# The order of five TensorE parts in a recurrence step: scores and masked product ahead of the state's product and the updates

## The reference, cut to what matters

```python
b_c = jnp.cumsum(_chunk(log_f), axis=3)
u = jnp.einsum('bhnck,bhncv->bhnkv', k_end, v_c)              # update of each chunk
s_next = d_n[..., None] * s + u_n                             # the state's chain over chunks
o_inter = jnp.einsum('bhnck,bhnkv->bhncv', q_c * jnp.exp(b_c), s_prev)
a = jnp.einsum('bhnck,bhnsk->bhncs', q_c * jnp.exp(b_c - b_mid), k_c * jnp.exp(b_mid - b_c))
a = jnp.where(jnp.tril(jnp.ones((CHUNK, CHUNK), dtype=bool)), a, 0.0)
o_intra = jnp.einsum('bhncs,bhnsv->bhncv', a, v_c)
return (o_inter + o_intra).reshape(b, h, t, -1)
```

## Time and profile before

| | |
|---|---|
| device time, median of 3 runs | 2343.97 us (2338.73 to 2344.09) |
| span of the profiled execution | 2340.7 us |
| PE busy | 2222.3 us, 95% |
| DVE busy | 1327.2 us, 57% |
| ACT busy | 864.2 us, 37% |
| POOL busy | 463.9 us, 20% |

### The profile page before, as it was taken

One profiled execution on the slowest core, in us unless ns is written; L12 is line 12 of the kernel. 1 busy time (PEld: TensorE's weight loads), 2 busy tenths in 40 slices (PEclk: granted clock), 3 DMA queues, 4 the chain that ended last, 5 costly groups with the idle time before them and its releaser, 6 DMA issues.

```text
span 2340.7 us, 33900 instructions
## 1 busy us (share of the span) xinstructions
PE 2222.3 (95%) x12064; PEld 1436.2 (61%) x12258; DVE 1327.2 (57%) x2357; ACT 864.2 (37%) x1888; POOL 463.9 (20%) x439
## 2 busy tenths in 40 slices
PE   5799999999999999999999999999999999998998
PEld 2566667666667666666666766656655555554554
DVE  6747547537637628628627727755554546364444
ACT  5734334334334424424424424444432221314221
POOL 2021221222222222222212221000043213100100
PEclk7899999999999999999999999999999999999999
DMA  6210110110011011010011010243321111113443
GB/s 256 83 39 28 35 39 28 33 41 28 26 46 30 26 43 33 26 43 32 22 46 35 21 46 21 84 160 130 132 72 36 62 41 41 50 41 131 135 135 117
DMA packets 106775, 144.80 MB, mean 62 GB/s; under 512 B 7136, under 2 KB 74224, under 8 KB 105584
## 3 DMA queue, kind: packets, MB, share of 16 engines
q1 hardware_dynamic: 99648, 125.72, 16.5%
q10 hardware_dynamic: 6960, 16.80, 1.9%
HBM read 108.91 MB, written 33.57 MB: 61 GB/s over the span
## 4 chain that ended last, share of the span: by engine, by line
PE 76%; DVE 9%; issue 8%; ACT 5%; DMA 1%; POOL 1%; SPq 0%; DVEq 0%; POOLq 0%; ACTq 0%
PE bank L1213 22%; PE bank L1211 21%; PE bank L1212 19%; DVE w_st L1040 2%; PE bank L1337 2%; PE bank L1445 2%; PE bank L1332 2%; PE bank L1352 2%; PE bank L1363 1%; PE bank L1305 1%; DVE xa L997 1%; ACT xb L667 1%; DVE qp L981 1%; DMA ada_sb<-in_ada_w 1%; ACT xb L681 1%
## 5 line engine op out<-in xcount | busy, mean ns | idle before, releaser
L1213 PE MATMUL bank<-h_hi,w_lo 128*128 128x512 f32 (+1 forms) x1472 | 815.9, 554 | 0.0
L1211 PE MATMUL bank<-h_hi,w_hi 128*128 128x512 f32 (+1 forms) x1472 | 578.9, 393 | 8.6 <-issue 7.1
L1212 PE MATMUL bank<-h_lo,w_bf 128*128 128x512 bf16 (+1 forms) x1343 | 505.2, 376 | 4.9 <-issue 4.9
L1212 PEld LDWEIGHTS bank<-h_lo,w_bf 128*128 128x128 bf16 x1472 | 142.0, 96 | 334.8 <-issue 318.3
L1211 PEld LDWEIGHTS bank<-h_hi,w_hi 128*128 128x128 f32 x1472 | 282.4, 192 | 39.2 <-issue 9.8
L1213 PEld LDWEIGHTS bank<-h_hi,w_lo 128*128 128x128 f32 x1472 | 297.8, 202 | 5.2 <-issue 5.2
L1213 PE MATMUL bank<-wo_hi,og_lo 128*128 128x512 f32 x512 | 299.4, 585 | 0.0
L649 ACT ACTIVATE xa<-bank 128x512 f32<-128x512 f32 (+1 forms) x144 | 82.5, 573 | 398.6 <-PE bank L1213 398.6
L1213 PE MATMUL bank<-h_hi,pw_lo_b 128*128 128x512 f32 x384 | 222.8, 580 | 0.0
L1211 PE MATMUL bank<-wo_hi,og_hi 128*128 128x512 f32 x512 | 205.2, 401 | 12.2 <-DVE wo_lo L1086 7.1
L1040 DVE SCALAR_TENSOR_TENSOR w_st<-w_st,cv,bank 128x128 f32<-128x128 f32 x560 | 193.4, 345 | 19.0
(11 more groups left out here) (163 smaller groups left out, 3807.2 us busy)
## 6 DMA issues: line engine op xcount, KB each, us to landing
w_raw<-in_w_in SPq DMA_DIRECT2D x80, 256.0 KB, 2.8
ada<-in_ada_late SPq DMA_DIRECT2D x128, 128.0 KB, 2.1
ada_sb<-in_ada_w SPq DMA_DIRECT2D x8, 1024.0 KB, 12.6
xt<-in_x SPq DMA_DIRECT2D x16, 512.0 KB, 6.5
gated_scratch<-o_t ACTq DMA_DIRECT2D x32, 256.0 KB, 2.4
og<-gated_scratch SPq DMA_DIRECT2D x16, 512.0 KB, 4.1
xr<-in_x SPq DMA_DIRECT2D x16, 512.0 KB, 4.9
x_scratch<-xr ACTq DMA_DIRECT2D x16, 512.0 KB, 2.6
```

What stands on the lines that cost most here:

```text
L1211: pe.matmul(out_ap, hi, m_hi, start=start, stop=False)
L1212: pe.matmul(out_ap, bf, m_lo, start=False, stop=False)
L1213: return pe.matmul(out_ap, lo, m_hi, start=False, stop=stop)
```

## The change: another order on PE

In a step PE's order becomes projection, T, A, M, O, U, output transposes. The scores are issued right behind the transposes. The masked product goes ahead of the state's product, so it now starts bank OB's accumulation (`start=(j == 0)`) and the state's product ends it (`stop=True`, and `o_done` behind it). Each part keeps its own waits: A's for the last masked copy, M's for its own masked copy and for bank OB to be read, O's for `q2` and the chain. No other engine's instructions change.

```diff
                         last.then_inc(s["kt_tr"], 1)
+                        if lat(fi) is not None:
+                            ai = lat(fi)
+                            need(pe, "a_masked", NA, h, ai)
+                            for j in range(4):
+                                last = pe.matmul(bank[AB][:, j * P:(j + 1) * P], kp[:, fi % 2, j * P:(j + 1) * P],
+                                                 qp[:, ai % 2, j * P:(j + 1) * P], start=(j == 0), stop=True,
+                                                 skip_group_check=True)
+                            last.then_inc(s["a_done"], 1)
                     fi = st - (F0 + 4)
...
+                        need(pe, "a_masked", NA, h, ai + 1)
+                        need(pe, "o_read", NA, h, ai)
+                        o = bank[OB]
+                        for j in range(4):
+                            pe.matmul(o[:, j * P:(j + 1) * P], am[:, 2 * d + ai % 2, j, :],
+                                      v_tok[:, 2 + 4 * b + j, :], start=(j == 0), stop=False,
+                                      skip_group_check=True)
                         need(pe, "q2_ready", NA, h, ai + 1)
                         need(pe, "w_step", NCHAIN, h, chain_steps(fi) - 1)
-                        need(pe, "o_read", NA, h, ai)
-                        o = bank[OB]
                         for n in range(8):
...
-                            pe.matmul(o[r, c // 2 * P:(c // 2 + 1) * P], q2[:, ai % 2, c * CHUNK:(c + 1) * CHUNK],
-                                      w_st[:, (8 * ai + n) % 16, :], start=(n < 2), stop=False,
-                                      skip_group_check=True)
-                        need(pe, "a_masked", NA, h, ai + 1)
-                        for j in range(4):
-                            last = pe.matmul(o[:, j * P:(j + 1) * P], am[:, 2 * d + ai % 2, j, :],
-                                             v_tok[:, 2 + 4 * b + j, :], start=False, stop=True,
+                            last = pe.matmul(o[r, c // 2 * P:(c // 2 + 1) * P],
+                                             q2[:, ai % 2, c * CHUNK:(c + 1) * CHUNK],
+                                             w_st[:, (8 * ai + n) % 16, :], start=False, stop=True,
                                              skip_group_check=True)
                         last.then_inc(s["o_done"], 1)
...
-                    fi = st - (F0 + 2)
-                    if 0 <= fi < NF:
-
-                        if lat(fi) is not None:
-                            ai = lat(fi)
-                            need(pe, "a_masked", NA, h, ai)
-                            for j in range(4):
-                                last = pe.matmul(bank[AB][:, j * P:(j + 1) * P], kp[:, fi % 2, j * P:(j + 1) * P],
-                                                 qp[:, ai % 2, j * P:(j + 1) * P], start=(j == 0), stop=True,
-                                                 skip_group_check=True)
-                            last.then_inc(s["a_done"], 1)
```

## The result

The changed kernel takes 2360.95 us (median of 4 runs, 2357.94 to 2361.86), the kernel before on the same chip 2344.03 us: a ratio of 1.0073, interval 1.006 to 1.0087. It is 17 us slower. I had said 2348.5 us, 2338 to 2359, and gave "slower" 0.36; the result lies outside the range on the slow side. The profiled execution has a span of 2355.8 us (2357.94 us of device time), 15.1 us more than the span before.

What follows compares the result with a forecast made beforehand. PE was taken to bound the run most of the time, with DVE's state chain holding it in places. A head sums to 0.73 - 0.6 + 0.45 = +0.58 us, eight to +4.6, on 2343.97: 2348.5 us, range 2338 to 2359.

Steps and rivals of the forecast that it cites:

- slower: The outcome of a time above 2351 us, with 0.3% (7 us) counted as no change; chance 0.36.
- The new wait: A waits for DVE's masked copy, starting 1.05 us later than O did; steps 14 and 15 cost +0.73 us a head.
- Fewer changes of shape: In a full step PE changes the array's shape three times instead of four, saving 0.22 us.
- O to U is free: Rival: PE's change of shape from O to U costs nothing; 2337.3 us, or 2335 with DVE freed; chance 0.12.
- Step 20: Its end comes +0.45 us later a head, between 0.14 (0.8 us of DVE freed) and 0.95 (DVE keeps its pace).
- U's later result "is hidden": U's result comes some 1 us later, but DVE starts the chain more than 5 us behind it, so no cost.
- The layers behind the heads are as before: The layers after the eight heads stay unchanged, except that they start later by the heads' sum, +4.6 us.
- The clock ... I take 0: The low clock behind step 14's longer idle time adds 0 us in sum, range -3 to +7.
- The first rival: Long low clock behind step 14 in all heads, +7 us, and DVE's pace kept in step 20, +4: 2359.5; chance 0.2.

Runs made afterwards that it cites:

- run with the wait alone: The kernel before, with the state's product O also waiting for the last masked copy in steps that have scores; 2360.79 us, ratio 1.0085.
- the run with extra work: The changed kernel with twelve extra matmuls in step 14 of each head, ahead of the scores' wait for the masked copy; 2347.66 us, ratio 1.0008.
- the scores first: The kernel before with only the scores A moved behind the transposes, O still ahead of M (order T, A, O, M, U); 2354.61 us, ratio 1.0044.
- the early copy alone: The kernel before with only DVE's masked copy moved ahead of the state's chain; 2351.06 us, ratio 1.0036.

## Why the prediction was wrong, point by point

- **The new wait: right.** A in step 14 starts 0.05 us behind the copy's end, O never waits for the chain, A(19) comes 9.88 us behind projection 18 (I said 9.9). Up to step 16 the heads cost +6.6 us in sum (3.9 + 5.5 - 2.8) against a forecast of 8 x 0.73 = 5.8. The wait in step 13 I had overlooked; it is taken up by the idle time of step 14. The run with the wait alone loses 18 us with nothing moved, so the wait carries a loss of this kind without the order.
- **Fewer changes of shape: right in size.** O before U takes 1.02 us, as one paid change (I had 1.03); the rival "O to U is free" falls. By the Trainium skill's rule ("TensorEngine Tiling (Array Packing)", Key Properties) a change of mode drains the engine, and the trace agrees in that half columns to half rows is paid as whole to half is. Step 16 saved 0.19 us (T(16) to T(17), 9.56 to 9.37) and step 17, which has all five parts, 0.18, where I had 0.22 for each.
- **Step 20: the lower bound held.** I took +0.45 us a head between 0.14 and 0.95. PE does not wait in step 20: the masked copies of steps 18 and 19 are 8.14 us apart where they had been 10.91, since POOL's `q2` starts at 964.00, 4 us behind the copy of step 18 (959.99), where it had followed at 2 us. T(19) to the next head's T costs 8.4 us less 1.1 for each end, so next to nothing.

```profile
959.99 0.72 DVE L1049 COPY_PREDICATED am<-mask,bank 128x512 f32<-128x512 uint8 x1
...
968.13 0.73 DVE L1049 COPY_PREDICATED am<-mask,bank 128x512 f32<-128x512 uint8 x1
```
```profile
964.00 1.58 POOL L555 TENSOR_TENSOR q<-qp,cv 128x512 f32<-128x512 f32 x1 [18.15 <-PE bank L1345]
```

- **U's later result "is hidden": not quite.** DVE's chain waits 12.0 us over 16 times for U in the changed kernel, since A, M and O run at the low clock ahead of it; in the run with extra work, where the clock stays up there, it waits 1.8 us over 8 times. It does not reach PE, which waits for nothing in step 15.
- **"The layers behind the heads are as before", and no term for the heads' ends: the step that failed.** I had read step 22 as T to T and O against M, saw the saving of 0.03 us and stopped there. The jump's idle time, 1.5 to 2.1 us in the trace of before with the engine waiting for nothing that the profile names, was before me, and so was the low clock behind two of five ends. I took the idle time as fixed and the term as nothing. In the two profiles the idle time grew by 0.7 us each (3.5 us), and the time behind it, with the low clock, by 9.9 us: 13.4 of the 15.1 us. The two runs that change the last part alone measured 5.5 and 6 to 8 us, which is about half of the distance from my 2348.5 to 2360.95. The rest of the 13.4 us lies at the same place in the two profiles, and its cause stays open.
- **"The clock ... I take 0": the same fault.** I had weighed the clock only behind step 14, where it did stay nearly the same (+2 us, forecast 0, range -3 to +7). The first rival gave 2359.5 us for a different place: a long low stretch behind every step 14 and DVE's pace kept in step 20, neither of which happened. The time came close to that rival by luck, from another cause.
- **What is left.** Without the jump the sum would have been +1.7 us in the profile (15.1 - 13.4), against my +4.6.

Still open: why the low clock behind the jumps is long in all five ends of the changed kernel, in three with its last step restored, and in none with the scores first (one short stretch), though the idle times with the last step restored and with the scores first are much alike (8.9 us against 9.2 in sum). Where the ends lie in time may decide it; no run shifted them alone. Chance has a part too: step 14 is the same in the changed kernel and in its version with the old last step, and T(14) to T(15) sums to 3.4 us more in the one profile than in the other. Nor is the last part all that sets the idle time: in the kernel with extra work, which has more PE instructions in its loop, it is one piece of 3.7 to 4.1 us. The last part accounts for about 6 us of the loss by the two runs that change it alone.

## What to carry to other kernels

Before you move a part on an in-order queue, look up what its own wait stands for on the other engine: a wait that was always met where it stood can be the last to be met where it goes, and all that is queued behind pays. Move the producer with it; here the whole new order alone lost 0.7% and the early copy alone 0.4%, and both gave 0.8%, 1.0% with the last step left as it was. Try the halves of a change too: the masked product first, alone, gained 0.4%. And read the end of a loop's body as a part of the loop: what came last there changed the idle time at the jump by 0.65 us of about 2, and behind such idle times, 1.5 to 2.8 us, the clock was often low for the work that follows.

## What the runs showed of the hardware that I had not expected

- The idle time at a loop's jump went with the part ahead of it: 1.5 to 2.1 us behind four whole-array products (35 jumps), 2.2 to 2.8 us behind eight half-array ones that take 1.02 us together (20 jumps); the kernel with extra work in its loop is apart, with 3.7 to 4.1 us. Why, no run shows.
- Extra matmuls can pay. Twelve of them in an idle time of 3.3 us kept the granted clock at 2.4 GHz behind it in all eight heads and made the kernel 13 us faster.
- Short idle times kept the clock: two of 0.9 and 0.5 us in step 14 were followed by no low clock in any head, one of 1.8 us by it in two heads of sixteen (the two kernels with the masked product first and the scores last), one of 2.7 us in seven of eight. No run cut one wait into pieces of the same sum.
- From the masked copy of step 18 to that of step 19 DVE takes 8.1 us or 10.9 us with the same instructions, depending on when POOL's `q2` and weight cuts run. The Trainium skill says that a DVE instruction with two SBUF inputs contends with GpSimd's reads ("SBUF — State Buffer", Who interferes with whom). The trace agrees for the products on two SBUF tiles: with POOL beside them line 984 takes 1.09 us instead of 0.68, line 992 1.77 instead of 0.68 and the small line 975 0.96 instead of 0.17, while the chain's links, with one input in PSUM, take 3.0 us for eight in both cases. But the copy of line 969, with one SBUF input, stretched as well, 0.64 us instead of 0.17, which that sentence does not cover. The four together are the whole difference of 2.8 us. In the changed kernel POOL's `q2` starts 0.01 us behind line 992, and there POOL is the one that takes longer, 1.58 us instead of 1.04.
